# Two blocks of a transformer on one core: low halves, row sums and group ends in another order

## The reference, cut to what matters

```
def first_block(x, c, ...):
    for i in range(2):
        mod = silu(c) @ ada_w[i] + ada_b[i]          # six rows of 1024 for each layer
        h = _rms(x) * (1.0 + sc1) + sh1
        y = _rwkv7_mix(h, ...) if i == 0 else _mlstm_mix(h, ...)
        x = x + g1 * y
        h = _rms(x) * (1.0 + sc2) + sh2
        x = x + g2 * _swiglu(h, ffn_w_gu[i], ffn_w_down[i])

def _mlstm_mix(x, ...):                              # 8 heads, 64 wide for q and k, 128 for v
    qk = silu(_causal_dwconv(p[..., :1024], conv_w, conv_b))
    ...                                              # gates, stabilised by the running maximum m_t
    den = max(abs(den), exp(-m_t))
    h = num / den
    h = h * rsqrt(mean(h * h, -1) + EPS) * hn_w
    return (h * sigmoid(o)) @ w_out

def mla_branch(h, ...):                              # 16 heads, q 128 + 64 rope, latents of 768 and 256
    q = (c_q @ w_uq); q_abs = q_nope @ w_uk; ...
    pr = softmax(where(causal, q_cat @ k_cat^T, -inf))
    o = (pr @ c_kv) @ w_uv
    return (silu(gate) * o) @ w_out
```

## Time and profile before

| | |
|---|---|
| median of three runs | 2438.64 us (2434.49 to 2443.08) |
| the profiled execution | 2435.84 us |
| its span, and clock granted to PE | 2434.0 us, 0.995 |
| PE busy | 2378.5 us, 98% |
| DVE, ACT, POOL busy | 1634.1, 1113.6, 523.3 us |

### The profile page before, as it was taken

One profiled execution on the slowest core, in us unless ns is written; L12 is line 12 of the kernel. 1 busy time (PEld: TensorE's weight loads), 2 busy tenths in 40 slices (PEclk: granted clock), 3 DMA queues, 4 the chain that ended last, 5 costly groups with the idle time before them and its releaser, 6 DMA issues.

```text
span 2434.0 us, 38419 instructions
## 1 busy us (share of the span) xinstructions
PE 2378.5 (98%) x16018; PEld 2014.7 (83%) x16018; DVE 1634.1 (67%) x2281; ACT 1113.6 (46%) x1671; POOL 523.3 (22%) x198
## 2 busy tenths in 40 slices
PE   8998989999999999999999999999999999999999
PEld 7747875798989888889898989999887778777787
DVE  6578768896868786488675696666617636777514
ACT  6663545352525445545353454322435435555533
POOL 1312203100000244520000002333134343111233
PEclk9999999999999999999999999999999999999999
DMA  7222344235354344124332323222222222112121
GB/s 297 87 91 66 76 116 180 84 124 189 122 176 170 111 158 138 62 87 148 121 113 88 122 93 120 77 80 70 79 89 102 94 102 102 55 70 70 61 87 69
DMA packets 94412, 264.29 MB, mean 109 GB/s; under 512 B 55200, under 2 KB 55840, under 8 KB 69280
## 3 DMA queue, kind: packets, MB, share of 16 engines
q1 hardware_dynamic: 91936, 253.46, 30.3%
q10 hardware_dynamic: 2304, 8.39, 0.9%
HBM read 256.05 MB, written 5.78 MB: 108 GB/s over the span
## 4 chain that ended last, share of the span: by engine, by line
PE 77%; DVE 11%; ACT 5%; issue 4%; DMA 2%; POOL 1%; SPq 0%; DVEq 0%; ACTq 0%
PE bank L357 13%; PE bank L359 13%; PE bank L358 13%; PE bank L2606 6%; PE bank L2608 6%; PE bank L2609 5%; PE bank L290 2%; PE bank L288 2%; PE bank L289 2%; ACT w_high L378 1%; PE bank L4723 1%; DMA ada_slot<-in_first 1%; PE bank L3321 1%; DVE conv_out L3557 1%; PE bank L4717 1%
## 5 line engine op out<-in xcount | busy, mean ns | idle before, releaser
L388 POOL TENSOR_TENSOR ring_low<-ring,w_high 128x2048 fp32r<-128x2048 f32 (+2 forms) x94 | 426.7, 4540 | 1672.3 <-ACT w_high L378 1672.3
L378 ACT ACTIVATE w_high<-ring 128x2048 fp32r<-128x2048 f32 (+1 forms) x128 | 234.8, 1840 | 227.9 <-PE bank L359 218.4
L357 PE MATMUL bank<-h_high,w_high 128*128 128x512 f32 (+1 forms) x480 | 192.3, 401 | 0.0
L359 PE MATMUL bank<-h_high,ring_low 128*128 128x512 f32 (+1 forms) x480 | 190.2, 396 | 0.0
L358 PE MATMUL bank<-h_low,w_high 128*128 128x512 f32 (+1 forms) x480 | 189.1, 394 | 0.0
L357 PE MATMUL bank<-z_high,w_high 128*128 128x512 f32 x380 | 151.6, 399 | 2.9 <-DVE z_low L4302 1.0
L359 PE MATMUL bank<-z_high,ring_low 128*128 128x512 f32 x380 | 150.3, 396 | 0.0
L358 PE MATMUL bank<-z_low,w_high 128*128 128x512 f32 x380 | 149.6, 394 | 0.0
L2609 PE MATMUL bank<-h_high,ring_low 128*128 128x256 f32 x528 | 147.2, 279 | 0.0
L357 PE MATMUL bank<-hidden_high,w_high 128*128 128x512 f32 x352 | 139.5, 396 | 0.0
L359 PE MATMUL bank<-hidden_high,ring_low 128*128 128x512 f32 x352 | 139.5, 396 | 0.0
(11 more groups left out here) (594 smaller groups left out, 6799.2 us busy)
## 6 DMA issues: line engine op xcount, KB each, us to landing
ring<-in_stream SPq DMA_DIRECT2D x186, 1024.0 KB, 4.8
ada_slot<-in_ada_next SPq DMA_DIRECT2D x40, 512.0 KB, 4.0
ada_slot<-in_gains SPq DMA_DIRECT2D x17, 512.0 KB, 4.5
ada_slot<-in_first SPq DMA_DIRECT2D x16, 512.0 KB, 4.4
scale_weights<-in_first SPq DMA_DIRECT2D x4, 1024.0 KB, 23.1
inverse<-scratch_inverse SPq DMA_DIRECT2D x32, 128.0 KB, 3.1
x_res<-in_x SPq DMA_DIRECT2D x2, 1024.0 KB, 9.0
w_first<-in_first SPq DMA_DIRECT2D x2, 1024.0 KB, 16.7
```

The source lines that it names most:

```text
L357: pe.matmul(out, w_high[:, k, cols], x_high, start=start, stop=False)
L359: return pe.matmul(out, w_low[:, k, cols], x_high, start=False, stop=stop)
L378: act.activation(self.high_buf[:, b % 2, 0:cols], self.c.ring[:, b % SLOTS, 0:cols], ACT.Copy)\
L388: pool.tensor_tensor(self.c.ring_low[:, b % SLOTS, 0:cols], self.c.ring[:, b % SLOTS, 0:cols], self.high_buf[:, b % 2, 0:cols].bitcast(F32 ...
```

## The change

Seven things are changed.

1. mLSTM: the low halves of fifteen blocks move from POOL to DVE, at places between the taps, the gate rows, the heads and the residual's tiles. The 18 rows are summed at other places; ten of them come before the heads, in two slots, and the last eight in the heads, one in each, in slot 1 alone.
2. mLSTM, last head: 12 of the 20 sums of head 7 come before the turn of head 6; POOL makes head 6's z_low before head 7's root; ACT rounds `b_w + 1` after head 6's z rather than in head 7.
3. Feed-forward: ACT seeds a group's bank before it rounds the weights of form 6.
4. Retention's first group: ACT seeds before the third silu.
5. Retention's end: the spread comes at n = 5 rather than 6.
6. MLA: the fourth head of a quarter turns and gathers its values in banks 4 to 7, and the next quarter's rope block is laid around its turns. In the last quarter tiles of the output projection take that place.
7. MLA: z is rounded and split a head or two sooner in the last quarter.

```
-def residual(chip, dve, b0, u0, gain, tail, second_half=None, behind_two=None):
+def residual(chip, dve, b0, u0, gain, tail, second_half=None, behind_two=None, split=None):
...
+        if split and n in (1, 3):
+            split.low(dve, b0 + 2 + n // 2)
...
                 seven.seed_b(act, d)
+                if d != firsts[p]:
+                    seven.high(act, d, 6)
...
-                if n is not None:
-                    seven.high(act, n, 6)
...
-    ROWS_BEHIND = {3: (0, 1), 4: (2,), 5: (3,), 6: (4,), 7: (5, 6), 8: (7, 8), 10: range(9, 15), 11: range(15, 18)}
+    ROWS_BEHIND = {3: (0, 1), 4: (2,), 5: (3,), 6: (4,), 7: (5, 6), 8: (7, 8), 9: (9,), 12: (10, 11), 13: (12, 13),
+                   14: (14, 15), 15: (16, 17)}
...
-            if hd:
+            if 0 < hd < H - 1:
                 turn(hd - 1)
-            sums(hd)
+            if hd < H - 1:
+                sums(hd)
+        sums(H - 1, 0, ST - 1)
+        turn(H - 2)
+        sums(H - 1, ST - 1, ST)
...
-            if hd % 2:
+            if hd % 2 and hd < H - 1:
                 split.high(act, b_o + hd // 2 + 2)
         copy_sums(H - 1)
         round_z(H - 2)
+        split.high(act, b_w + 1)
...
+            if n == KD - 1:
+                split.low(dve, b_v)
...
-            if n % 2:
+            if n % 2 and n < KD - 1:
+                split.low(dve, b_qk + n // 2 + 2)
                 take_rows(1)
+        take_rows(1)
+        split.low(dve, b_v + 1)
         take_rows(3)
...
         weigh(0)
-        take_rows(1)
         for hd in range(H):
             if hd:
                 normalise(hd - 1)
+            if hd and hd % 2 == 0:
+                split.low(dve, b_o + hd // 2 + 1)
+            if hd % 2 and hd < H - 1:
+                take_rows(1)
             if hd + 1 < H:
                 weigh(hd + 1)
+            if hd == 0:
+                split.low(dve, b_o + 1)
             if hd:
                 gated(hd - 1)
+            if hd % 2 == 0:
+                take_rows(1)
         normalise(H - 1)
+        split.low(dve, b_w + 1)
+        take_rows(1)
         gated(H - 1)
...
-            if n == 6:
+            if n == 5:
                 spread_rstd(RH - 1)
...
             if d == 0:
-                for t in range(3):
+                for t in range(2):
                     silu_of(t)
             seven.seed_c(act, d)
+            if d == 0:
+                silu_of(2)
...
+        if hd % 4 == 3:
+            bank, first = {0: (4, 0), 1: (5, P), 2: (6, 0), 3: (5, 0)}[i]
...
+    def values_bank(hd):
+        return chip.bank[7 if hd % 4 == 3 else 2 + hd % 2]
...
+        def latent_tile(b, u, j):
+            w = split.parts(b, QT, 2 * P)
+            for k in range(QT):
+                mm = three(pe, chip.pair(u)[j][:, :], w, k, tok(j), latent_parts(k), k == 0, k == QT - 1)
+            mm.then_inc(chip.gemm_done, 1)
+
+        def rope_block(qt, between=None):
+            b, u = quarters[qt]
+            split.wait(pe, b)
+            chip.wait_pair(pe, u)
+            first, second = (1, 0) if qt and u % 2 else (0, 1)
+            latent_tile(b, u, first)
+            if between:
+                between()
+                pe.wait_ge(z_ready.sem, z_ready.of(4 * qt - 2))
+            latent_tile(b, u, second)
...
+            hd = 4 * qt + 3
+            if qt < 3:
+                b, u = quarters[qt + 1]
+                rope_block(qt + 1, between=lambda: turns(hd))
+                values(hd)
+                chip.pe_features(pe, b + 1, u + 1, 1, QT, latent_parts, split=split)
+            else:
+                assert u_o % 2 == 0
+                split.wait(pe, b_o)
+                chip.wait_pair(pe, u_o)
+                out_tile(0, 0, 0, 2)
                 turns(hd)
+                out_tile(0, 0, 2, 3)
                 values(hd)
+                out_tile(0, 0, 3, H)
...
-                if qt == 3 and a >= 2:
-                    round_z(2 * a - 4)
-                    round_z(2 * a - 3)
+                if qt == 3 and a:
+                    round_z(2 * a - 2)
+                    round_z(2 * a - 1)
```

More of the change, by code:

```diff
@@ L3213, in mlstm @@
     here = [chip.tally(f"ada_here{s}") for s in range(2)]
-    here_base = [t.take(16 * len(rows) // 2) for t in here]
+    early = len(rows) - H
+    here_base = [t.take(16 * n) for t, n in zip(here, (early // 2, early // 2 + H))]
     ada_sum = Step(chip, "ada_sum", len(rows))
@@ L3309, in scores, with sums @@
             score(chip.bank[6][:, 0:P], 2, 3 * P, far).then_inc(s_mm[2].sem, 1)
-        def sums(hd):
-            pe.wait_ge(wt.sem, wt.of(3 * hd + 2))
-            if hd:
-                pe.wait_ge(nd_copy.sem, nd_copy.of(2 * (hd - 1)))
-            chip.wait_pair(pe, u_o + hd // 2 + 1)
-            if hd >= 2:
-                pe.wait_ge(z_mul.sem, z_mul.of(hd - 2))
-            for j in range(ST):
+        def sums(hd, first=0, last=ST):
+            if first == 0:
+                pe.wait_ge(wt.sem, wt.of(3 * hd + 2))
+                if hd:
+                    pe.wait_ge(nd_copy.sem, nd_copy.of(2 * (hd - 1)))
+                chip.wait_pair(pe, u_o + hd // 2 + 1)
+                if hd >= 2:
+                    pe.wait_ge(z_mul.sem, z_mul.of(hd - 2))
+            for j in range(first, last):
                 out = last_bank(hd)[:, 0:W] if j == ST - 1 else chip.bank[7][:, j * W:(j + 1) * W]
@@ L3677, in gpsimd @@
         pool.tensor_scalar(hn[:, :], chip.v("hn_w"), 0.5, None, ALU.mult).then_inc(half.sem, 1)
-        for n in range(2, 9):
-            split.low(pool, b_qk + n)
         mask(0)
-        split.low(pool, b_o)
         mask(1)
-        split.low(pool, b_o + 1)
         for hd in range(H):
@@ L4661, in tensor @@
         kv_norm.wait(pe, CT - 1)
-        for qt in range(4):
+        def latent_tile(b, u, j):
[4 more added lines that the diff above has]
+        def rope_block(qt, between=None):
             b, u = quarters[qt]
@@ L4666, in tensor, with out_tile @@
             chip.wait_pair(pe, u)
-            w = split.parts(b, QT, 2 * P)
-            for j in range(2):
-                if qt and u % 2 and j:
-                    pe.wait_ge(z_ready.sem, z_ready.of(4 * qt - 1))
-                for k in range(QT):
-                    mm = three(pe, chip.pair(u)[j][:, :], w, k, tok(j), latent_parts(k), k == 0, k == QT - 1)
-                mm.then_inc(chip.gemm_done, 1)
-            if qt and u % 2 == 0:
-                pe.wait_ge(z_ready.sem, z_ready.of(4 * qt - 1))
-            chip.pe_features(pe, b + 1, u + 1, 2, QT, latent_parts, split=split)
+            first, second = (1, 0) if qt and u % 2 else (0, 1)
[4 more added lines that the diff above has]
+            latent_tile(b, u, second)
+        def out_tile(r, tile, first, last):
+            parts = split.parts(b_o + 2 * r + tile, H, P)
+            for n in range(first, last):
+                if r == 0 and tile == 0:
+                    pe.wait_ge(z_rest.sem, z_rest.of(n))
+                mm = three(pe, chip.pair(u_o + r)[tile][:, :], parts, n, slice(0, P),
+                           (z_high[:, n, :], z_low[:, n, :]), n == 0, n == H - 1)
+            if last == H:
+                mm.then_inc(chip.gemm_done, 2)
+        for qt in range(4):
+            b, u = quarters[qt]
+            if qt == 0:
+                rope_block(0)
+                chip.pe_features(pe, b + 1, u + 1, 1, QT, latent_parts, split=split)
+            chip.pe_features(pe, b + 2, u + 2, 1, QT, latent_parts, split=split)
             split.wait(pe, b + 3)
@@ L4698, in scores @@
                 a = hd % 4
+                if hd and a == 0:
+                    pe.wait_ge(z_ready.sem, z_ready.of(hd - 1))
                 for j in range(first, last):
@@ L4742, in tensor @@
                     pe.wait_ge(raised.sem, raised.of(12 * qt + 11))
+                if a < 3:
+                    turns(hd)
+                    if a < 2:
+                        scores(hd + 1, 2, ST)
+                    values(hd)
[3 more added lines that the diff above has]
+                rope_block(qt + 1, between=lambda: turns(hd))
+                values(hd)
+                chip.pe_features(pe, b + 1, u + 1, 1, QT, latent_parts, split=split)
+            else:
+                assert u_o % 2 == 0
+                split.wait(pe, b_o)
+                chip.wait_pair(pe, u_o)
+                out_tile(0, 0, 0, 2)
                 turns(hd)
-                if a < 2:
-                    scores(hd + 1, 2, ST)
+                out_tile(0, 0, 2, 3)
                 values(hd)
-        assert u_o % 2 == 0
+                out_tile(0, 0, 3, H)
         for r in range(4):
             for tile in range(2):
+                if r == 0 and tile == 0:
+                    continue
                 split.wait(pe, b_o + 2 * r + tile)
@@ L4752, in tensor @@
                     chip.wait_pair(pe, u_o + r)
-                parts = split.parts(b_o + 2 * r + tile, H, P)
-                for n in range(H):
-                    if r == 0 and tile == 0:
```

(7 more changed lines are left out.)

46 lines of the change are left out of this document (24 added, 22 removed).

## The result

| | before | after |
|---|---|---|
| median (lowest to highest), 8 runs each | 2438.07 us (2434.43 to 2443.08) | 2422.56 us (2420.1 to 2432.6) |
| the profiled execution, its span | 2435.84, 2434.0 us | 2424.09, 2422.3 us |

The ratio is 0.9938, with a 95% interval of 0.9925 to 0.9951: 15 us less, between 12 and 18. The profiled executions differ by 11.75 us, as the forecast said for them (2424.2 against 2424.09), and the medians by 15.5. So the sum for the profiled execution came out, and that for the median was 4 us short. That the first agrees to 0.1 us is chance: RWKV, which the change leaves alone, took 2.9 us more in the profiled execution after. Both have to be read by stretches.

A forecast was written before the change was run, and what follows sets the result against it. TensorE, busy 2378.5 of 2434.0 us, was taken as the bound, so only its holes could be won: 4.1 + 1.0 + 0 + 1.2 + 5.3 = 11.6 us, from a median of 2438.64 to 2427.0 us, range 2420 to 2437.

The forecast's parts named there:

- The four holes of 4.83 us: mLSTM: PE's waits of 1.80, 1.22 and 0.68 us for POOL's low halves and 1.13 for its z_low all go.
- the turn's 1.09: mLSTM: PE's 1.09 us wait before head 6's turn, covered by 12 sums of head 7; 0.5 us taken as gain.
- The loop: mLSTM's head loop: busier DVE makes the next chain late, worse if POOL's mask holds its low half; 1.2 us lost.
- the rule on two SBUF inputs: mLSTM: a two-SBUF-input DVE operation and a GpSimd operation reading SBUF exclude each other; each low holds POOL up to 2.28 us.
- Seedings: Feed-forward group's end: seeding sooner removes PE's 1.07 us wait for ACT's copy; 1.0 us gained (0.9 to 1.3).
- Retention's seed: Retention's first group: the 1.04 us wait for ACT's seed goes, but PE waits longer for DVE's join; 0 gained.
- MLA, 5.3 expected: MLA: covered turns gain four times 1.32, plus 0.6 at the projection, less 0.6; 5.3 us (2.5 to 6.5).
- the loss of 0.6 for rotations behind the gating: MLA: DVE's fourth-head gating now just precedes turning the next quarter's queries; 0.2 us lost in each of three quarters.
- A: mLSTM's head loop is bound by DVE and costs 8 us in place of 1.2; time 2433.8; chance 0.13.
- B: MLA's 1.3 us wait reappears at the next quarter's rotations or scores, half the gain lost; 2429.6; chance 0.12.
- C: mLSTM's last eight rows, sharing one slot, land late and delay every head behind; 2446 us; chance 0.07.
- D: mLSTM: the moves to DVE do nothing, the 4.83 us stay, and B holds too; 2433.7; chance 0.10.

The follow-up runs named there:

- low_after_weigh: Changed kernel with VectorE's low half in heads 2, 4 and 6 behind the weighing of the next head's scores; head 0's turn to last sum 60.60 us against 60.63.
- m_only: Kernel before with only the mLSTM edits (items 1 and 2); ratio 0.9975, median 2429.72 us, mLSTM stretch 233.21 us.
- a_only: Kernel before with only the MLA edits (items 6 and 7); ratio 0.9975, median 2429.0 us, embedding and MLA stretch 541.83 us.
- order_only: Kernel before, low halves still on GpSimd, with 12 of head 7's sums before head 6's turn and z_low before head 7's root; mLSTM 237.37 us.
- rest_only: Kernel before with only the seedings and the spread (items 3 to 5); one execution, 2436.44 us, retention stretch 423.85 us.
- join_first: Changed kernel with VectorE's join ahead of the gate product in retention's first group; ratio 0.9933 to the kernel before, median 2420.4 us.
- no_cover: Changed kernel with MLA's new banks but TensorE's old order at the quarters' ends; embedding and MLA stretch 547.56 us, 5.0 more.
- dose1: Changed kernel with one more 1.2 us VectorE operation in each even head of mLSTM, ahead of the row's sum; mLSTM 238.19 us, 4.7 more.

## Why the prediction was right, and where it was off

The median of 2422.56 us lies in the range, but at its lower end and 0.1 us under the best case by the bounds (2422.7): the mechanisms were right, and the terms of doubt were nearly all too pessimistic.

- **mLSTM, 4.1 us expected, 5.6 found** (5.8 alone). The four holes of 4.83 us went as worked out, and the turn's 1.09 went whole where I had taken 0.5. The loop was put at 1.2 us and cost 0.26, in head 0 alone, which my reckoning had left out. The mis-sized term is the hold: I let POOL's mask hold DVE's low half back. It was the other way round; the row took 1.21 us, not the 1.45 of a mean in which held ones were counted; and the next chain began only 0.3 us behind ACT's copies, which the spare of 0.48 took up. The lower bound given for this term, -6, counts the best case for the turn; by its own parts it is 4.83 - 12 = -7.2.
- The Trainium skill, page "SBUF — State Buffer", section "Who interferes with whom", says of the ports that DVE and GpSimd share that they are an exclusive lock and that issue order decides who blocks. The trace agrees: the low half started 0.01 us ahead of the mask, and a mask of 0.64 us took 2.77., which the prediction took for the rule on two SBUF inputs, show a hold too, but of a tap that reads one tensor and a scalar for each partition. What the rule can't tell is who waits for the one that is held, and here that was nobody, as low_after_weigh shows.
- **Seedings, 1.0 expected, 1.9 found** (0.95 in feed-forward 0, 0.93 in feed-forward 1). I had counted one hole, because the profiled execution of before shows 1.07 in one feed-forward and 0.30 in the other. m_only, a_only and order_only have 1.07 to 1.08 in the first. One execution's hole was taken for the kernel's. It varies in the second too: m_only has 0.68 there.
- **Retention's seed, 0 expected, 0 found.** The step was right: the join was the second bound, and rest_only shows the same 1.47 us without the other edits. DVE's chain ends it, as join_first shows.
- **Retention's end, 1.2 expected, 1.4 found.** The hole of 1.19 us went, and with it 0.2 us of smaller waits around it, which have no bracket.
- **MLA, 5.3 expected, 5.1 found** (5.85 alone). The four times 1.32 came, and the projection's wait too. The mis-sized term is the loss of 0.6 for rotations behind the gating: it was 0 in a_only. In the changed kernel 0.35 us stand at one pair wait and 0.3 at a block of the embedding, and these are a side effect of the mLSTM part: m_only and no_cover have both. The longer wait in the embedding (0.51 to 0.55 us) is in every kernel with the mLSTM part, and in none without it (0.22 or 0.23). By what path an edit 800 us earlier does this is open.
- **Rivals.** A (the loop bound by DVE) did not happen, but dose1 puts it close: 1.2 us more in each even head and 4.7 of the 5.6 are lost. B did not happen: even the 0.35 us is not the MLA edit's. C (rows late) has no trace even with 2.4 us more. D is refuted by m_only.
- **The median.** 14.0 us in the changed stretches, 15 by the ratio, against 11.6: of the 2.4 between the first and the last 1.5 is mLSTM's and 0.9 the seedings', and the 1 us left lies within the interval.

## What to carry to other kernels

When work moves to an engine that is faster at it, ask of each place who of the two will be held, and who waits for that one; a hold that nobody waits for costs nothing, and the place to look is how far behind the end of that engine's work its next chain begins. A hole that waits for a chain is best closed with work that PE has to do anyway, but count what of the cover the old hole uses up. The size of a hole in one execution is not its size in the kernel: take it from two profiles before it becomes a term, and compare profiles by stretches that the edit touches. Then look once at the stretches it does not touch, in a kernel with that edit alone: here two waits grew by 0.3 us each, 800 us and more behind the edit that brought them.

## What the runs showed of the hardware

In mLSTM's head loop PE's granted clock fell behind brackets of 1.96 to 2.62 us, and behind one of 3.73, and stayed at 1.00 behind those of 1.48 and less. The cost came on top of the hole: 4.5 us over three holes of about 2 us, 1.6 behind the one of 3.73. The size of the hole alone does not decide it, though. In a_only's RWKV, where PE makes other matmuls, it stayed at 1.00 behind 1.98 us (PE's timeline, then the window behind it):

```profile
268.78 1.15 PE L1555 MATMUL bank<-inverse,level 64*64 64x64 f32 x32 [1.98 <-DMA inverse<-scratch_inverse]
```

```profile
268.80:276.00 7.20, 7.20 (x198) 6.77 (x200) 6.54 (x13) 4.13 (x9) 0.00 (x0) 1.00 0.49 161
```
 The lower level shows in some executions, and not in others, in the statistics between phases, where PE does small transposes: at 822 to 828 us the granted clock is 1.00 in one profile and 0.72 in another. This costs 1.3 to 3.0 us a time. It and RWKV's stretch, 462.6 to 474.8 us, are where executions of these kernels differ most.
